# Routing in the merge stage: the router reads the un-normed rows, and its work moves one unit of tiles earlier

## The chip, the cores and the metric

The kernel runs on one core of a Trainium2 chip. The metric is device time in microseconds (us) of one execution; the time before is the median of 3 runs. Engines are named as in the profile: PE is TensorE, DVE VectorE, ACT ScalarE, POOL GpSimd, SP SyncE, which here only issues DMAs.

## The reference

One transformer layer over 1024 prompt rows and 32 sample rows, all float32. Attention and a linear recurrence give two branch outputs o_a and o_b of 512 columns each; they are projected to 1024 columns, gated, and added to x. Then comes a two-level mixture of 32 experts. The part that the change touches is this:

```
proj  = einsum('blnc,ncd->blnd', branches, w_out)
gates = sigmoid(gate_logits)
x  = x + sum(gates * proj, over the 2 branches)
h2 = rmsnorm(x, norm_ffn_g)               # x * rsqrt(mean(x*x) + eps) * g
g_prob = softmax(h2 @ w_rg + b_rg);  g_top, g_idx = top_k(g_prob, 1)
e_logits = h2 @ w_re + b_re;  e_top, e_idx = top_k(e_logits of that group, 2)
e_w = softmax(e_top) * g_top              # weights of the two experts
x  = x + sum over the two experts of e_w * ffn_e(h2)
```

## The kernel before

The program is written out by hand, engine by engine: each engine has its own list in program order, and semaphores (`wait_ge`, `then_inc`) tie them. An instruction that waits holds up all that stands behind it on its engine. The stages follow one another: inputs, mixing, attention, merge, experts.

**The merge** handles 9 tiles of 128 rows. Tile 0 is the tail with the sample rows, tiles 1 to 8 are the prompt. For tile t, PE turns the branch outputs (`turn_o`, L1920), and multiplies them in four units (`project(t, u)`, L1947) of four 512-column matmuls (float32, so each shows as two in the trace). DVE multiplies each unit by its gate (L1720) and adds it to x (L1722); the add of unit 3 raises `x_done`. ACT then sums the squares of x (L1868), DVE scales and adds epsilon (L1744), ACT takes the root (L1870), DVE the reciprocal (L1746) and writes h2 = x * r * g (L1749, `h2_ready`). PE turns h2 (`turn_h2`, L1956), DVE and ACT each copy half of the turned tile from PSUM (L1753, L1874), PE computes 36 logits per row (`router`, L1963), DVE picks the group and the experts (`choose`, L1759 to L1784), PE counts rows per expert before each row (`count`, L1970 to L1980), and DVE turns that into places (`record`, L1791 to L1804). After the last tile `finish_table` (L1810 to L1814) gives the row numbers from which POOL gathers the experts' rows of h2.

**Order on PE** in the loop (L1997): project(t,0), count(t-2), project(t,1), turn_h2(t-1), turn_o(t+1), project(t,2), router(t-1), project(t,3). The router of tile t-1 thus runs inside tile t.

**Order on ACT** (L1893): the squares and root of tile t-1, the sigmoid of the gates of tile t+1 (`sigmoid`, L1863, over 2048 columns), the copy of the turned h2, the copy of the turned branch outputs of tile t+1 (L1858), and `weights(t-1)` (L1879, L1881).

**Gates.** There are two gate buffers. The gates of tile t+1 go into the buffer of tile t-1, so SP loads them (L1628, 1 MB) only after `x_done` of tile t-1, right behind the store of that x (L1637). SP then waits for h2 and stores it (L1641), loads a later x (L1633), in tiles 1 to 3 the weights of an expert (L1644, L1647, 3 MB), and the branch outputs of a later tile (L1621, L1624). After the last projection and the last store of h2 it issues the weights that go into memory the merge used: 2 MB and three times 1 MB.

**The experts** start with gathers by indirect DMA (L2189), issued by POOL once the row numbers stand; PE turns the gathered rows and runs 32 experts.

## Time and profile before

| | us |
|---|---|
| three runs | 1634.65, 1632.19, 1633.59 |
| median | 1633.59 |
| span of the profiled execution | 1634.6 |
| that execution's own time | 1634.65 |
| merge: first turning to row numbers | 1105.5 to 1287.9 |
| PE busy over the whole span | 1502.0 (92%) |

The span starts with the first instruction and ends with the last. Times in the rows are microseconds from its start. In a timeline a bracket at the end of a row tells how long the engine sat idle before it and what released it. The profiled execution is the first of the three runs.

### The profile page before, as it was taken

Reading aid. Unit: us, or ns where it says so; the run is one execution under the profiler, and the core shown is the slowest. Engines: PE = TensorE matmul, PEld = TensorE weight load, DVE = VectorE, ACT = ScalarE, POOL = GpSimd, SP = SyncE. Lnnn points to the kernel's source line nnn. Section 1 sums busy time; section 2 is a strip of 40 time slices with the busy share of each in tenths; the row PEclk is TensorE's granted clock in tenths of the full one; section 3 lists DMA queues with packets and bytes.
Section 4 is the critical chain, followed back from the end, with each engine's and each line's share of the span. In section 5 each row is a group of like instructions: output and inputs, shape, how many; then the busy total and the mean of one; then the engine's idle time right before and its main releaser. Section 6 shows DMA issues by size and latency. Waiting matters only on the chain. (4 is left out here: it accounts for less than half of the span.)

```text
span 1634.6 us, 38777 instructions
## 1 busy us (share of the span) xinstructions
PE 1502.0 (92%) x16352; PEld 1064.2 (65%) x16352; DVE 857.1 (52%) x1874; ACT 446.4 (27%) x882; POOL 102.1 (6%) x102
## 2 busy tenths in 40 slices
PE   6999999969999999999999599988999599999994
PEld 5888888844666666666667466663455477777762
DVE  3555554545566667676776566663777323221211
ACT  2222222223222332333231144433543211111110
POOL 0000000000000000000000000000000122333321
PEclk9999999979999999999999699998999699999998
DMA  9422221544141232212112424436963799999972
GB/s 339 166 91 94 90 90 64 197 139 159 60 128 64 87 94 88 66 62 83 59 47 73 115 61 95 102 77 229 373 231 130 268 313 339 343 346 360 343 244 42
DMA packets 101326, 259.55 MB, mean 159 GB/s; under 512 B 34240, under 2 KB 53328, under 8 KB 91824
## 3 DMA queue, kind: packets, MB, share of 16 engines
q1 hardware_dynamic: 93424, 239.92, 42.8%
q0 software_dynamic: 7744, 17.33, 4.5%
q8 instruction: 124, 2.03, 0.5%
q14 instruction: 34, 0.28, 0.1%
HBM read 205.32 MB, written 60.56 MB: 163 GB/s over the span
## 5 line engine op out<-in xcount | busy, mean ns | idle before, releaser
L540 PEld LDWEIGHTS a_ps<-a_hT,a_wz 128*128 128x128 f32 x1792 | 202.6, 192 | 6.3 <-issue 3.8
L540 PE MATMUL a_ps<-a_hT,a_wz 128*128 128x128 f32 x1792 | 204.1, 275 | 1.8 <-DMA a_wz<-w_z 1.8
L1947 PE MATMUL d_ps<-late,last_down 128*128 128x512 f32 x256 | 115.4, 598 | 1.5 <-DVE last_down L1711 0.8
L2313 DVE TENSOR_SCALAR f_y<-f_down,table 96x512 f32<-96x512 f32 x32 | 23.9, 747 | 123.0 <-PE f_down L2108 70.8
L2115 DVE COPY f_xT<-f_turned 128x384 f32<-128x384 f32 x32 | 17.9, 558 | 123.8 <-PE f_turned L2082 121.2
L1947 PEld LDWEIGHTS d_ps<-late,last_down 128*128 128x128 f32 x256 | 46.7, 190 | 51.5 <-issue 50.2
L1120 PE MATMUL b_ps<-r_wg,r_hT 128*128 128x512 f32 x128 | 66.0, 650 | 12.1 <-POOL b_S L778 10.1
L1472 ACT ACTIVATE late<-c_score,c_top 128x1024 f32<-128x1024 f32 (+8 forms) x72 | 50.7, 704 | 92.8 <-DVE c_top L1421 92.0
L840 DVE TENSOR_TENSOR b_M<-b_ps,r_causal 128x512 f32<-128x512 f32 x72 | 46.4, 686 | 54.8 <-PE b_ps L1181 54.3
L1120 PE MATMUL b_ps<-b_wg,b_hT 128*128 128x512 f32 x128 | 64.2, 624 | 0.9 <-DMA b_hT<-hT_d 0.9
L1120 PE MATMUL b_ps<-b_wg,r_hT 128*128 128x512 f32 x128 | 63.1, 615 | 0.0
L2108 PE MATMUL f_down<-wd,f_midT 128*96 128x512 f32 x136 | 61.3, 593 | 1.8 <-DVE f_midT L2127 1.8
L1271 PE MATMUL b_solve<-b_L,b_U 64*64 64x32 f32 x1408 | 57.1, 222 | 5.7 <-DVE b_L L916 5.4
L1120 PE MATMUL b_ps<-r_wg,b_hT 128*128 128x512 f32 x128 | 62.1, 611 | 0.0
L1271 PEld LDWEIGHTS b_solve<-b_L,b_U 64*64 64x64 f32 x1408 | 51.3, 136 | 13.6 <-DVE b_L L916 6.5
L2320 ACT ACTIVATE f_xT<-f_turned 128x384 f32<-128x384 f32 x32 | 15.7, 492 | 159.7 <-PE f_turned L2082 156.4
L916 DVE TENSOR_TENSOR b_L<-b_solve,r_merge_mask 128x256 f32<-128x256 f32 x44 | 18.7, 424 | 75.3 <-PE b_solve L1255 75.3
L452 ACT ACTIVATE a_z<-a_ps 128x512 f32<-128x512 f32 (+1 forms) x36 | 19.6, 544 | 140.9 <-PE a_ps L540 134.1
L1255 PEld LDWEIGHTS b_solve<-b_T,b_M 64*64 64x64 f32 x1408 | 44.5, 134 | 18.4 <-issue 7.8
L2338 ACT ACTIVATE f_y<-f_down,table 96x512 f32<-96x512 f32 x32 | 21.9, 686 | 126.4 <-PE f_down L2108 73.6
L1519 PE MATMUL c_turned<-c_ident,late 128*128 128x128 f32 (+1 forms) x304 | 49.9, 290 | 6.3 <-ACT late L1472 6.3
L2232 POOL DMA_INDIRECT out<-f_y,rows x32 | 46.3, 1446 | 142.9 <-DVE f_y L2313 139.2
(373 smaller groups left out, 2928.5 us busy)
## 6 DMA issues: line engine op xcount, KB each, us to landing
wgu<-w_gate_up SPq DMA_DIRECT2D x15, 2048.0 KB
late<-w_gate_up SPq DMA_DIRECT2D x9, 2048.0 KB
wd<-w_down SPq DMA_DIRECT2D x17, 1024.0 KB
late<-w_down SPq DMA_DIRECT2D x10, 1024.0 KB
r_hT<-hT_d SPq DMA_DIRECT2D x18, 512.0 KB, 4.0
b_hT<-hT_d SPq DMA_DIRECT2D x18, 512.0 KB, 4.0
gate_d<-b_logits SPq DMA_DIRECT2D x32, 256.0 KB, 2.6
late<-gate_d SPq DMA_DIRECT2D x8, 1024.0 KB, 5.7
```

Of the source, the lines that this page charges most:

```text
L540: mm = pe.matmul(banks[Z_BANKS[n % 2]][:, j * P:(j + 1) * P], wz[:, i, (g + j) * P:(g + j + 1) * P], hT[t % 2][:, i, :], start=(i == 0), s ...
L840: ins = dve.tensor_tensor(m[:, 2 * p + j], banks[(C0, C1)[j]][:].rearrange("p (a b) -> p a b", a=2), spread(causal[:].unsqueeze(1), [P, 2, ...
L1120: mm = pe.matmul(banks[FILLS[q % 2]][:], hT[q % 2][:, k, :], wg[u % 2][:, k, :], start=(k == 0), stop=(k == DC - 1))
L1255: mm = pe.matmul(solve[half, s // 4, s % 4 * Q:s % 4 * Q + Q], m[half, h, 0, half], left, start=True, stop=True)
L1271: mm = pe.matmul(out(1), u[half, s, :], lo[half, s, 0:Q], start=True, stop=True)
L1472: act.activation(probs[b][:, 0:width[s]], score[b][:].rearrange("p a n -> p (a n)")[:, 0:width[s]], ACT.Exp, bias=top[:, b:b + 1], accum_o ...
L1519: mm = pe.transpose(turned[banks_of(p)[n // 4]][0:m, n % 4 * P:(n % 4 + 1) * P], probs[b][:, n * P:n * P + m], ident[:])
L1947: mm = pe.matmul(banks[2 + u][:], oT[t % 2][:, HB * branch(u) + k, :], wo[:, HB * branch(u) + k, half(u)], start=(k == 0), stop=(k == HB - 1))
L2108: mm = pe.matmul(down[h][0:CAP, :], midT[b][:, k, :], wd[wb][:, k, 512 * h:512 * h + 512], start=(k == 0), stop=(k == FB - 1))
L2232: pool.indirect_dma_start(out_rows, bass.IndirectOffsetOnAxis(ap=rows[:, ORDER[e]:ORDER[e] + 1], axis=0), y[e % 2][:], None, bounds_check= ...
L2313: dve.tensor_scalar(y[e % 2][:, 512:], down[1][0:CAP, :], weights[:, ORDER[e]:ORDER[e] + 1], None, ALU.mult).then_inc(s["y_dve"], 1)
L2338: act.activation(y[e % 2][:, 0:512], down[0][0:CAP, :], ACT.Copy, scale=weights[:, ORDER[e]:ORDER[e] + 1]).then_inc(s["y_act"], 1)
```

## The change

The router no longer reads h2. In `merge`, at its start, DVE multiplies the router's weights by the norm's gain g (one instruction over 288 columns; g comes as columns, by one more small DMA). PE turns x itself (`turn_x`, L1973 of the new file) as soon as `x_done` is raised; the row's factor r is applied to the logits when DVE adds the bias (L1766). h2 is still computed, for the experts, in `norm` (L1754), but nothing on PE waits for it. `mean_square` is split from `norm`, so that `record(t-2)` runs between the two.

The weights of the two experts are computed with Exp alone: with d = e_top[1] - e_top[0], the first is 1 / ((1 + exp d) * sum) and the second that times exp d. Before, Sigmoid was used. A one-element Exp stands first in `weights`.

The orders are rewritten. On PE the turning of x(t-1) comes behind project(t,0), the router of t-1 behind project(t,1), and the count of t-1 at the end of tile t. For the last tile, turning goes to the PSUM banks 0 and 1, and the count of tile 7 stands in the middle of project(8,3).

PE in the middle of the merge, one tile of the loop, before (names: `late` and `last_down` hold the output weights and the turned branch outputs, `seventh` x or h2, `unit` the identity):

```order
L1947 MATMUL d_ps<-late,last_down 128x512 x8
L1970 MATMUL d_ps<-d_both,m_before 128x32
L1971 MATMUL d_ps<-d_both,d_ones 128x32
L1980 MATMUL d_ps<-d_told,d_at_place 96x64 x2
L1947 MATMUL d_ps<-late,last_down 128x512 x4
L1956 MATMUL d_ps<-unit,seventh 128x128 x8
L1920 MATMUL d_ps<-unit,late 128x128 x8
L1947 MATMUL d_ps<-late,last_down 128x512 x4
L1963 MATMUL d_ps<-m_wr,d_h2T 64x36 x16
```

The same engine and place after the change:

```order
L1961 MATMUL d_ps<-late,last_down 128x512 x4
L1973 MATMUL d_ps<-unit,seventh 128x128 x8
L1961 MATMUL d_ps<-late,last_down 128x512 x4
L1980 MATMUL d_ps<-m_wr,d_xT 64x36 x16
L1932 MATMUL d_ps<-unit,late 128x128 x8
L1961 MATMUL d_ps<-late,last_down 128x512 x8
L1988 MATMUL d_ps<-d_both,m_before 128x32
L1989 MATMUL d_ps<-d_both,d_ones 128x32
L1998 MATMUL d_ps<-d_told,d_at_place 96x64 x2
```

The same instructions are there. Turning has moved ahead of project(t,1); between turning and the router there stands project(t,1), where turn_o(t+1) and project(t,2) stood before.

ACT in one tile of the loop, before (L1870 is the root, L1863 the sigmoid of the gates, L1874 the copy of the turned tile):

```order
L1870 ACTIVATE d_ms<-d_ms 128x1
L1863 ACT_TABLE_LOAD
L1863 ACTIVATE late<-late 128x2048
L1874 ACTIVATE d_h2T<-d_ps 128x512
L1858 ACTIVATE last_down<-d_ps 128x512
L1879 ACTIVATE d_small<-d_small 128x2
L1881 ACT_TABLE_LOAD
L1881 ACTIVATE d_gexp,d_small<-d_lg,d_small 128x4
L1866 ACT_TABLE_LOAD
L1866 ACTIVATE d_root_ready<-d_ones 128x1
```

And after:

```order
L1880 ACTIVATE d_ms<-d_ms 128x1
L1873 ACT_TABLE_LOAD
L1873 ACTIVATE late<-late 128x2048
L1885 ACTIVATE d_xT<-d_ps 128x512
L1868 ACTIVATE last_down<-d_ps 128x512
L1889 ACT_TABLE_LOAD
L1889 ACTIVATE d_exp_ready<-d_ones 128x1
L1891 ACTIVATE d_gexp,d_small<-d_lg,d_small 128x4
L1893 ACTIVATE d_small<-d_small 128x1
L1876 ACT_TABLE_LOAD
L1876 ACTIVATE d_root_ready<-d_ones 128x1
```

The copy of the turned tile keeps its place behind the sigmoid; the table load for Exp now stands before any wait of `weights`.

PE at the end of the merge, after the change, from project(8,3):

```order
L1961 MATMUL d_ps<-late,last_down 128x512 x6
L1988 MATMUL d_ps<-d_both,m_before 128x32
L1989 MATMUL d_ps<-d_both,d_ones 128x32
L1998 MATMUL d_ps<-d_told,d_at_place 96x64 x2
L1961 MATMUL d_ps<-late,last_down 128x512 x2
L1973 MATMUL d_ps<-unit,seventh 128x128 x8
L1980 MATMUL d_ps<-m_wr,d_xT 64x36 x16
```

Before, the count of tile 7 stood behind all of project(8,3). The core of the diff:

```diff
@@ SP
             def load_x(t):
                 after(sp, x_stored[t % 3], 16 * (t // 3))
                 after(sp, h2_ready, t - 2)
+                after(sp, xT_done, t - 2)
@@ DVE
-            def norm(n):
+            def mean_square(n):
                 col = ms[:, n:n + 1]
                 dve.wait_ge(x_sq, n + 1)
                 dve.tensor_scalar(col, col, 1.0 / D, EPS, ALU.mult, ALU.add).then_inc(ms_ready, 1)
+
+            def norm(n):
+                col = ms[:, n:n + 1]
                 dve.wait_ge(rms_root, n + 1)
                 step(dve.reciprocal(col, col))
                 after(dve, h2_stored[n % 2], 16 * (n // 2))
-                after(dve, h2T_done, n - 1)
...
-                dve.tensor_tensor(lg[:], banks[6][:, 0:RT], br[:], ALU.add).then_inc(lg_copied, 1)
+                after(dve, g_sum, n)
+                dve.scalar_tensor_tensor(lg[:], turned_into(n)[0][:, 0:RT], ms[:, n:n + 1], br[:], ALU.mult, ALU.add).then_inc(lg_copied, 1)
...
             mix_tail()
+            step(dve.tensor_tensor(wr[:], wr[:], spread(g_cols[:].unsqueeze(2), [P, DC, RT]), ALU.mult))
             copy_oT(1)
...
             for t in range(2, NT):
                 step.lap()
+                mean_square(t - 1)
+                record(t - 2)
                 norm(t - 1)
-                if t == 2:
-                    record(0)
                 unit(t, 0)
-                if t > 2:
-                    record(t - 2)
+                copy_xT(t - 1)
                 unit(t, 1)
-                copy_h2T(t - 1)
                 if t + 1 < NT:
                     copy_oT(t + 1)
+                choose(t - 1)
                 unit(t, 2)
-                choose(t - 1)
+                if t == NT - 1:
+                    record(t - 1)
                 unit(t, 3)
+            mean_square(NT - 1)
+            copy_xT(NT - 1)
             norm(NT - 1)
-            record(NT - 2)
-            copy_h2T(NT - 1)
             choose(NT - 1)
             record(NT - 1)
@@ ACT, weights(n)
-                act.wait_ge(d_ready, n + 1)
-                act.activation(sm[:, 6:8], sm[:, 4:6], ACT.Sigmoid).then_inc(d_sig, 1)
+                act.activation(exp_ready[:], ones[:, 0:1], ACT.Exp)
                 act.wait_ge(neg_top, n + 1)
                 act.activation(gexp[:], lg[:, 0:NG], ACT.Exp, bias=sm[:, 0:1], accum_out=sm[:, 1:2]).then_inc(g_sum, 1)
+                act.wait_ge(d_ready, n + 1)
+                act.activation(sm[:, 6:7], sm[:, 5:6], ACT.Exp).then_inc(d_exp, 1)
@@ PE
-            def turn_h2(n):
-                pe.wait_ge(h2_ready, n + 1)
-                after(pe, counted, n)
-                after(pe, lg_copied, n)
+            def turn_x(n):
+                pe.wait_ge(x_done, n + 1)
+                if n < NT - 1:
+                    after(pe, counted, n)
+                    after(pe, lg_copied, n)
+                else:
+                    pe.wait_ge(oT_copied, 2 * NT)
...
             project(1, 1)
+            turn_x(0)
             project(1, 2)
-            turn_h2(0)
+            router(0)
             project(1, 3)
-            router(0)
```

## Rows read from the trace of the kernel before

**Rows 1.** The page: the chain that ended last, by line

```profile
PE f_down L2108 7%; PE d_ps L1947 6%; PE f_gated L2097 6%; PE f_upped L2097 5%; PE f_turned L2082 2%; PE d_ps L1956 1%; PE d_ps L1963 1%; PE d_ps L1920 0%; PE d_ps L1928 0%; DMA xg<-h_d,rows 0%; PE d_ps L1980 0%; DMA late<-oa_d 0%; DVE seventh L1749 0%; ACT L1866 0%
```

**Rows 2.** The chain in order of time, one tile: start us, us, what

```profile
1217.42 3.49 PE d_ps L1947 x8
1220.91 0.78 issue
1221.69 1.06 PE d_ps L1956 x8
1222.76 0.87 PE d_ps L1920 x8
1223.63 3.44 PE d_ps L1947 x8
1227.06 1.06 PE d_ps L1963 x32
1228.12 7.06 PE d_ps L1947 x16
...
1235.92 3.49 PE d_ps L1947 x8
```

**Rows 3.** DVE's timeline: start us, us, line, operation, [idle before]

```profile
1159.26 0.69 DVE L1722 TENSOR_TENSOR seventh<-seventh,d_mixed 128x512 f32<-128x512 f32 x1
...
1214.13 0.69 DVE L1722 TENSOR_TENSOR seventh<-seventh,d_mixed 128x512 f32<-128x512 f32 x1
...
1250.99 0.69 DVE L1722 TENSOR_TENSOR seventh<-seventh,d_mixed 128x512 f32<-128x512 f32 x1
...
1268.47 0.69 DVE L1722 TENSOR_TENSOR seventh<-seventh,d_mixed 128x512 f32<-128x512 f32 x1
```

**Rows 4.** ACT's timeline

```profile
1151.29 1.91 ACT L1863 ACTIVATE late<-late 128x2048 f32<-128x2048 f32 x1 [4.58 <-DMA late<-gate_d]
...
1220.92 1.92 ACT L1863 ACTIVATE late<-late 128x2048 f32<-128x2048 f32 x1 [1.91 <-DMA late<-gate_d]
1222.79 0.60 ACT L1874 ACTIVATE d_h2T<-d_ps 128x512 f32<-128x512 f32 x1
...
1270.48 1.04 ACT L1868 ACTIVATE d_junk<-seventh 128x1024 f32<-128x1024 f32 x1
```

**Rows 5.** SP's timeline: DMA issues

```profile
1273.95 0.43 SPq L1644 DMA_DIRECT2D late<-w_gate_up  x1
```

**Rows 6.** Issue to landing, gates issued at 1125.01, then at 1215.24

```profile
late<-gate_d SPq DMA_DIRECT2D x1, 1024.0 KB, 5.4
...
late<-gate_d SPq DMA_DIRECT2D x1, 1024.0 KB, 5.7
```

**Rows 7.** The chain in order of time, end of the merge

```profile
1272.27 1.30 DVE seventh L1749
...
1274.44 1.95 PE d_ps L1956 x8
...
1277.23 1.95 PE d_ps L1963 x32
...
1279.20 0.21 DVE d_lg L1759
...
1282.71 0.64 PE d_ps L1970 x2
...
1284.51 0.20 DVE d_pos L1795
...
1287.72 0.19 DVE rows L1814
...
1288.90 4.34 DMA xg<-h_d,rows
```

**Rows 8.** Stretches: us, busy by engine, PEclk (granted clock), DMA share, GB/s

```profile
1268.00:1269.20 1.20, 0.90 (x8) 0.76 (x8) 1.13 (x2) 1.17 (x4) 1.20 (x2) 1.00 0.00 0
1280.00:1288.00 8.00, 2.63 (x12) 2.29 (x12) 4.96 (x28) 1.88 (x4) 0.00 (x0) 0.50 0.99 421
```

More of the change, by code:

```diff
@@ L1562, in merge @@
         wo, begun = keep["wo"], keep["begun"]
-        wr, br, ident, before, g_ffn, count_up, real, token, places, nobody, fold = (begun[n] for n in "wr br ident before g_ffn count_up real token places nobody fold".split())
+        wr, br, ident, before, g_ffn, count_up, real, token, places, nobody, fold, g_cols = (begun[n] for n in "wr br ident before g_ffn count_up real token places nobody fold g_cols".split())
         ones = sb("ones", [P, P])
@@ L1747, in norm, with copy_xT @@
                 after(dve, h2_stored[n % 2], 16 * (n // 2))
-                after(dve, h2T_done, n - 1)
                 dve.scalar_tensor_tensor(h2[n % 2][:], x[n % 3][:], col, g_ffn[:], ALU.mult, ALU.mult).then_inc(h2_ready, 1)
-            def copy_h2T(n):
-                dve.wait_ge(h2T_done, n + 1)
-                dve.tensor_copy(h2T[:, 4:, :], banks[7][:].rearrange("p (a b) -> p a b", b=P)).then_inc(h2T_copied, 1)
+            def copy_xT(n):
+                dve.wait_ge(xT_done, n + 1)
+                after(dve, lg_done, n)
+                dve.tensor_copy(xT[:, 4:, :], turned_into(n)[1][:].rearrange("p (a b) -> p a b", b=P)).then_inc(xT_copied, 1)
             def choose(n):
@@ L1790, in record @@
                 dve.wait_ge(g_sum, n + 1)
-                step(dve.reciprocal(sm[:, 3:4], sm[:, 1:2]))
-                dve.wait_ge(d_sig, n + 1)
-                dve.tensor_scalar(rec[:, 2 * NE + 4:], sm[:, 6:8], sm[:, 3:4], None, ALU.mult)
+                dve.wait_ge(d_exp, n + 1)
+                step(dve.scalar_tensor_tensor(sm[:, 3:4], sm[:, 6:7], 1.0, sm[:, 1:2], ALU.add, ALU.mult))
+                step(dve.reciprocal(rec[:, 2 * NE + 4:2 * NE + 5], sm[:, 3:4]))
+                dve.tensor_tensor(rec[:, 2 * NE + 5:], rec[:, 2 * NE + 4:2 * NE + 5], sm[:, 6:7], ALU.mult)
                 dve.wait_ge(count_done, n + 1)
@@ L1824, in _ @@
             unit(1, 1)
+            mean_square(0)
             norm(0)
             copy_oT(2)
+            copy_xT(0)
             unit(1, 2)
-            copy_h2T(0)
             unit(1, 3)
@@ L1870, in norm, with copy_xT @@
                 act.activation(ms[:, n:n + 1], ms[:, n:n + 1], ACT.Sqrt).then_inc(rms_root, 1)
[L1872 to L1874 removed]
+            def copy_xT(n):
+                act.wait_ge(xT_done, n + 1)
+                after(act, lg_done, n)
+                act.activation(xT[:, 0:4, :], turned_into(n)[0][:].rearrange("p (a b) -> p a b", b=P), ACT.Copy).then_inc(xT_copied, 1)
             def weights(n):
                 sm = small[n % 2]
[L1878 to L1879 removed]
+                act.activation(exp_ready[:], ones[:, 0:1], ACT.Exp)
                 act.wait_ge(neg_top, n + 1)
                 act.activation(gexp[:], lg[:, 0:NG], ACT.Exp, bias=sm[:, 0:1], accum_out=sm[:, 1:2]).then_inc(g_sum, 1)
+                act.wait_ge(d_ready, n + 1)
+                act.activation(sm[:, 6:7], sm[:, 5:6], ACT.Exp).then_inc(d_exp, 1)
             sigmoid(0)
@@ L1936, in fold_tail, with project @@
                 mm.then_inc(fold_done, 1)
-            def project(t, u):
+            def project(t, u, between=None):
                 pe.wait_ge(oT_copied, 2 * (t + 1))
@@ L1946, in project @@
                 for k in range(HB):
+                    if k == HB // 2 and between is not None:
+                        between()
                     mm = pe.matmul(banks[2 + u][:], oT[t % 2][:, HB * branch(u) + k, :], wo[:, HB * branch(u) + k, half(u)],
@@ L1968, in count @@
                 pe.wait_ge(both_ready, n + 1)
-                pe.wait_ge(h2T_copied, 2 * (n + 1))
+                pe.wait_ge(xT_copied, 2 * (n + 1))
+                after(pe, counted, n)
                 pe.matmul(banks[7][:, 0:NE], before[:], both[:], start=True, stop=True)
@@ L1992, in _ @@
             project(1, 1)
+            turn_x(0)
             project(1, 2)
-            turn_h2(0)
+            router(0)
             project(1, 3)
-            router(0)
             for t in range(2, NT):
-                project(t, 0)
-                count(t - 2)
+                if t == 2:
+                    project(t, 0, lambda: count(0))
+                else:
+                    project(t, 0)
+                turn_x(t - 1)
                 project(t, 1)
-                turn_h2(t - 1)
+                router(t - 1)
                 if t + 1 < NT:
@@ L2004, in _ @@
                 project(t, 2)
-                router(t - 1)
-                project(t, 3)
-            count(NT - 2)
-            turn_h2(NT - 1)
+                if t == NT - 1:
+                    project(t, 3, lambda: count(NT - 2))
+                else:
+                    project(t, 3)
+                    count(t - 1)
+            turn_x(NT - 1)
             router(NT - 1)
```

35 lines of the change are left out of this document (17 added, 18 removed).

## The prediction

> **What bounds the kernel now.** I read the page's chain first [rows 1]: it is nearly all PE, in the experts (L2082, L2097, L2108) and in the merge (L1947 and the turning and routing lines). The change touches only the merge and the start of the experts, so I read the chain there in order of time [rows 2]. One tile lasts from 1217.42 to 1235.92, 18.50 us. Of that 0.78 is a hole ahead of the turning (L1956); the rest, 17.72, is PE at work: four units of about 3.5, turning 1.06, turning o 0.87, routing 1.06, and by difference 0.74 for the count. DVE's adds of unit 3 end (start plus 0.69) at 1159.95 for tile 2 and 1251.68 for tile 7 [rows 3], so five tiles took 91.73, or 18.35 each. The reader should see that PE is 96% full there: all that a better order can win in a tile of the loop is about 0.65 us.
>
> Next come the engines that PE waits for. On ACT the sigmoid of the next tile's gates starts at 1220.92 and was released by the DMA of the gates; the copy of the turned tile follows it at 1222.79 and ends at 1223.39 [rows 4]. Routing started only at 1227.06 [rows 2]: 3.6 us of slack.
>
> Last, the end of the merge [rows 3, 7]: x of tile 8 is complete at 1269.16, the row numbers stand at 1287.91. These 18.75 us are a chain without overlap: squares on ACT from 1270.48 [rows 4], h2, turning 1.95, copy, routing 1.95, choose, count, record. PE's granted clock is 1.00 before and 0.50 in this stretch, the lower level of 1.2 GHz [rows 8], which is why turning takes 1.95 and not 1.06.
>
> **The loop.** PE's instructions per tile stay the same, 17.72 us. What goes is the hole: turning needs `x_done` and the count's release instead of h2. With t0 the moment of `x_done` (PE's last unit ends 1.45 before it, for two DVE instructions of 0.7), PE does the count 0.74 and project(t,0) 3.53, and wants to turn at t0+2.8. DVE's release (`counted`) comes after squares 1.25, mean 0.2 and the first half of record, about 1.1: t0+2.6. No hole there, or a very small one.
>
> Then comes project(t,1), 3.49, and PE wants to route at t0+7.4. The turned tile must have been copied by both engines. DVE gets there after record 2.1, norm 1.5, one unit 1.45 and the copy 0.7, at about t0+7.1. ACT does not. Its copy still stands behind the sigmoid, and the sigmoid behind the gates, whose load cannot be issued before t0, since their buffer is that of tile t-1. From `x_done` at 1214.82 the sigmoid started 6.10 later [rows 3, 4], the load having taken 5.7 from issue [rows 6]. After the change h2 is stored later, so the gates have the queue to themselves as at 1125.01, where the load took 5.4: 5.80. Then sigmoid 1.87, copy 0.60 and a signal 0.05: routing starts at t0+8.3. The slack of 3.6 is used up because turn_o and project(t,2), 4.3 together, no longer stand in front of routing; PE waits about 0.95.
>
> So the tile becomes a ring through the DMA: 8.32, routing 1.06, turn_o 0.87, two units 3.44 and 3.53, and 1.45 to the next `x_done`: 18.67, against 18.35. Five tiles (3 to 7) cost 5 x 0.32 = 1.6 us instead of winning 3. The bounds of the landing are the two rows, 5.4 and 5.7: ring 18.67 to 18.97, or 1.6 to 3.1 in all; below, I allow 0.2 less landing for a queue quieter still, 0.6. I take 1.6.
>
> **The first tiles.** The gates of tile 3 landed so that the sigmoid ran at 1151.29 [rows 4]; their load stood behind 3 MB of expert weights, which are issued after h2 of tile 0, a step that is not moved. So this time stays. The copy ends at 1153.8, where routing began before too. But then turn_o and project(2,2) had been done, now they come after it. `x_done` of tile 2 is 1153.80+1.06+0.87+3.44+3.53+1.45 = 1164.15 instead of 1159.95: +4.2. The longer wait for choose(0) ahead of the count inside project(2,0), about 3.6, lies in the shadow of these gates. Bounds: +2.7 if the queue is emptied earlier by 1.5, +5.7 if later.
>
> **The last tile of the loop** has no gates to load: 17.6 us from `x_done` to `x_done`, now with the count of tile 7 inside, against 17.5 (1251.68 to 1269.16). Together `x_done` of tile 8 comes 4.2+1.6+0.1 = 5.9 later.
>
> **The end.** From `x_done` of tile 8: squares 1.25, mean 0.2, root 0.25, ACT's copy 0.6, routing 1.06 end at 3.4; DVE meanwhile copies 0.7, takes the reciprocal 0.2 and writes h2 1.3 [rows 7], free at 3.6. Choose takes what it took from 1279.20 to 1282.71, 3.5; the count until 1284.51, 1.8; the rest until 1287.91, 3.4. Sum 12.3 against 18.75: 6.45 won. It is what stood in series before: turning, one of its copies and h2, the Exp with its table load ahead of the squares (ACT began them at 1270.48, 1.3 after x was there), and turning and routing at the lower clock. PE now rests about 1.5 us before turning, so I take 1.06 for each. If the clock falls all the same, 0.9 comes back on the routing; if it stays at 1.00 through the count as well, 1.3 more is won.
>
> **The start.** One DVE multiply over 288 columns stands ahead of the copy of turned branch outputs; scaled from 0.69 for 512 columns it takes 0.4, of which some lies in a short wait. I take 0.2, bounds 0 and 0.4. The constant's DMA lies under attention, at nothing; if that cover were missing it would be one small load before the merge.
>
> **The gather.** The weights into freed memory, 5 MB, are issued once h2 of tile 8 is stored. Before, that was 1273.95 [rows 5], and at 421 GB/s and a DMA share of 0.99 [rows 8] they were through as the gather began at 1288.90, which landed 4.34 later [rows 7]. Now the store comes 3.6 after `x_done` instead of 4.4, and the row numbers 12.3 after it instead of 18.75. The gather begins 5 to 6 us before the weights are through. Lower bound nothing; upper bound: it waits for them all, landing at 18.9+3.2 = 22.1 after `x_done` instead of 17.6, +4.5. I take 2.0, nearer the lower end, for the gather is small (96 rows) and on another queue.
>
> The Trainium skill, "DMA: Bandwidth & Descriptors", section "Queues, rings and completion order", says that each DMA engine goes round among its queues, one packet at a time. By that rule the gather shares instead of waiting, which favours the lower half of my bounds; no row here shows a gather's landing beside a full weight queue.
>
> **Sum.** Start +0.2, tiles +5.9, end -6.45, gather +2.0: +1.65. The profiled execution took 1634.65, 1.06 above the median of the three, so the sum is 1636.3 on its scale and 1635.2 on the median's. The experts behind carry it one for one: their weight loads are released by their own steps.
>
> Another page bears on the end. Rows show the table loads as 1.28 each, with the next instruction right behind. The Trainium skill, "ScalarE: Activation LUTs", section "What ACT_TABLE_LOAD costs", gives 2.66 for every switch, a drain of 1.38 included. By it, taking a load out of the end would win 1.38 more, 1633.8 in all. The rows disagree and decide.
>
> **Rivals.** First, faster: the gates do not hold PE. It would need the copy ready at t0+7.4, a landing 0.95 shorter than the 5.4 seen; then five waits go, -4.8, and the median is 1630.4, or 1628.4 with a free gather. For it: 1.5 MB are moved, and the queue is quieter; against it: even the undisturbed load took 5.4. Second, slower: the gather waits for the weights to the end, +2.5 on my term, 1637.7. For it: the share of 0.99 over the whole stretch; it decides as soon as more than 4.3 us of weights stand before the gather. Third, slower: the gates of tile 4 or 5 queue behind the 3 MB of weights that are now issued later, after the later h2. Those weights need about 12 us from some 5 after `x_done`, and the next `x_done` comes at 18.7, so about 1.5 us are to spare; if that is gone one or two tiles lose 1 to 3 us, 1638.0. Fourth, the change does not do what it says: `counted` comes late and turning is not earlier. It has a margin of 0.2 only, but a delay below 0.95 vanishes in the wait for the gates, so this gives the forecast's time.
>
> **How the numbers follow.** Forecast 0.52 (the fourth rival is in it), first rival 0.18, second 0.16, third 0.14. A measurement of this kernel tells about 0.2%, 3.3 us, from no change: 1630.3 to 1636.9. The forecast's own range is 1632 to 1638; I count 0.42 of it as same, 0.08 as slower, 0.02 as faster. The first rival gives faster 0.14 and same 0.04; the second slower 0.12, same 0.04; the third slower 0.10, same 0.04. Rounded: faster 0.17, same 0.53, slower 0.30. The range of 1629.5 to 1639.5 takes in the upper half of the first rival and nearly all of the others.
>
> **What would show it.** In the trace after: L1980 (routing) on PE has a wait of about 1 us in tiles 3 to 7 that ends with ACT's copy L1885, itself right behind the sigmoid L1873 released by the DMA of gates; no hole before L1973; the adds of unit 3 lie 18.7 apart; routing of tile 1 starts near 1153.8; from the last such add to the row numbers 12.3 us; the first gather lands more than 5 us after its start. I am wrong if routing starts right behind project(t,1), or if the end saves less than 5 us.

## The result and the profile after

The changed kernel takes 1642.42 us, median of 6 runs (1638.67 to 1647.53); the kernel before, run beside it, 1633.74 (1628.85 to 1634.88). The ratio is 1.0063, with a 95% interval of 1.0048 to 1.0078: slower by 8.7 us by the medians and by 10 by the ratio, where no measurable change was forecast. It lies above the range of 1629.5 to 1639.5. The profiled execution took 1642.85, its span is 1641.0.

All stretches below are counted from the start of `project(1, 0)`, the first full unit of the merge (1117.76 before, 1113.32 after). Of the change only the multiply lies ahead of it: it runs 0.45 us (1112.09), and PE's wait there is 0.99 instead of 0.78. Otherwise this start varies between single executions: in the profiles of all kernels here it lies between 1112.7 and 1117.8. So absolute times of two profiles can't be compared. From there to the end the profiles show 516.84 us before and 527.68 after, 10.8 more; the two spans differ by only 6.4, since the part ahead happened to be 4.4 shorter in the second.

The page of the profile, the chain by line, answers to [rows 1]. New in it, against the kernel before, are the DMA of the gates and ACT's copy:

```profile
PE f_down L2131 7%; PE f_gated L2120 6%; PE f_upped L2120 5%; PE d_ps L1961 5%; DMA late<-gate_d 2%; PE f_turned L2105 2%; PE d_ps L1980 1%; PE d_ps L1932 0%; DMA xg<-h_d,rows 0%; PE d_ps L1940 0%; DVE d_mixed L1723 0%; DVE seventh L1725 0%; ACT d_xT L1885 0%; DMA late<-oa_d 0%
```

The chain in order of time (start us, us, what) over one tile, the answer to [rows 2]. L1725 is the last add of a unit (`x_done`), L1640 and `late<-gate_d` the store of x and the load of the gates, L1885 ACT's copy, L1980 routing, L1932 `turn_o`:

```profile
1201.04 0.70 DVE seventh L1725
...
1201.76 0.34 SPq L1640
...
1202.14 5.63 DMA late<-gate_d
...
1207.91 1.71 issue
1209.61 0.59 ACT d_xT L1885
...
1210.25 1.13 PE d_ps L1980 x32
1211.38 1.02 PE d_ps L1932 x8
1212.40 6.88 PE d_ps L1961 x16
...
1219.38 0.70 DVE d_mixed L1723
...
1220.10 0.70 DVE seventh L1725
```

This is the ring that the prediction describes, from one `x_done` to the next through the gates' DMA: 19.06 us, where [rows 2] have 18.50 with PE at work. (The 1.71 of "issue" is the sigmoid, which runs from 1207.80.) DVE's timeline, the last add of tiles 2, 3, 7 and 8, answers to [rows 3]:

```profile
1161.48 0.69 DVE L1725 TENSOR_TENSOR seventh<-seventh,d_mixed 128x512 f32<-128x512 f32 x1
...
1182.18 0.69 DVE L1725 TENSOR_TENSOR m_x<-m_x,d_mixed 128x512 f32<-128x512 f32 x1
...
1258.29 0.69 DVE L1725 TENSOR_TENSOR seventh<-seventh,d_mixed 128x512 f32<-128x512 f32 x1
...
1275.72 0.69 DVE L1725 TENSOR_TENSOR seventh<-seventh,d_mixed 128x512 f32<-128x512 f32 x1
```

Tile 3 took 20.70, the four behind it 19.03 each, (1258.29 - 1182.18) / 4. PE's timeline with its waits (start us, us, line, [idle before <- releaser]) shows what happened up to tile 3:

```profile
1130.10 1.15 PE L1980 MATMUL d_ps<-m_wr,d_xT 128*64 128x36 f32 x32 [1.81 <-ACT d_xT L1885]
...
1141.93 0.63 PE L1988 MATMUL d_ps<-d_both,m_before 128*128 128x32 f32 x2 [3.70 <-DVE d_both L1791]
...
1142.80 3.76 PE L1961 MATMUL d_ps<-late,last_down 128*128 128x512 f32 x4
1146.36 1.92 PE L1973 MATMUL d_ps<-unit,seventh 128*128 128x128 f32 x8
...
1151.63 1.13 PE L1980 MATMUL d_ps<-m_wr,d_xT 128*64 128x36 f32 x32
...
1170.64 1.13 PE L1980 MATMUL d_ps<-m_wr,d_xT 128*64 128x36 f32 x32 [1.46 <-ACT d_xT L1885]
1171.70 1.70 PE L1932 MATMUL d_ps<-unit,late 128*128 128x128 f32 x8
```

PE waited 1.81 ahead of routing(0) and 3.70 inside `project(2, 0)` for choose(0). Four matmuls behind the second wait took 3.76, half a unit, which at full speed is 1.8; turning took 1.92 instead of 1.04. The same behind the wait of 1.46: `turn_o` 1.70 instead of 1.09. The windows (us, busy by engine, granted clock, DMA share, GB/s) show what changed there:

```profile
1130.00:1134.00 4.00, 3.90 (x36) 2.28 (x37) 0.00 (x0) 1.53 (x3) 0.00 (x0) 0.63 1.03 392
...
1140.00:1148.00 8.00, 6.07 (x16) 3.90 (x17) 5.87 (x26) 5.86 (x8) 0.00 (x0) 0.58 0.59 233
...
1172.00:1174.00 2.00, 2.00 (x9) 1.53 (x8) 0.50 (x1) 0.56 (x1) 0.00 (x0) 0.51 0.96 356
...
1180.00:1268.00 88.00, 82.10 (x423) 44.31 (x422) 60.72 (x196) 39.77 (x62) 0.00 (x0) 1.00 0.50 179
```

The granted clock fell from 1.00 (2.4 GHz) to 0.50 (1.2 GHz) for a few us behind these three rests, and not behind the four of 1.3 to 1.6 that came later. The kernel before rests 1.85 us at 1145.8 and keeps 1.00 behind it, so the length of a rest alone does not decide it. Last, the end of the merge in the chain, the answer to [rows 7]:

```profile
1277.93 0.59 ACT d_xT L1885
1278.57 1.95 PE d_ps L1980 x32
1280.55 0.27 DVE d_lg L1766
...
1284.11 0.64 PE d_ps L1988 x2
...
1285.91 0.20 DVE d_pos L1803
...
1289.13 0.19 DVE rows L1822
...
1290.31 7.69 DMA xg<-h_d,rows
```

and SP's timeline there, the answer to [rows 5]:

```profile
1279.83 0.32 SPq L1644 DMA_DIRECT2D h_d<-seventh  x1
1280.19 0.43 SPq L1647 DMA_DIRECT2D late<-w_gate_up  x1
```

Row numbers stand 12.9 us after the last `x_done` (18.75 before). But the late weights (5 MB) are issued 10.1 us before the gather instead of 15.0, and the gather takes 7.69 instead of 4.34. The windows show what runs beside it, at its start and its end:

```profile
1290.00:1292.00 2.00, 0.00 (x0) 0.00 (x0) 0.00 (x0) 0.00 (x0) 1.39 (x2) 0.50 1.01 426
...
1296.00:1298.00 2.00, 0.00 (x0) 0.00 (x0) 0.00 (x0) 0.00 (x0) 0.00 (x0) 0.50 0.79 189
```

By an estimate the weights, if nothing else ran, would be through some 4 us after the gather's start (5.77 MB with h2's store, at 421 GB/s [rows 8] 13.7 us from the issue at 1279.83, and some 0.7 until the first bytes in the trace of the DMA engines: 1294.2). Counted by queue in steps of 0.5 us, the gather's first bytes move 4.0 to 4.5 us after its start, against 1.5 to 2.0 in the kernel before; the weights' last ones move 5.0 to 5.5 after it.

The account over the stretches, in us against before:

| stretch | forecast | measured |
|---|---|---|
| multiply, ahead of `project(1, 0)` | +0.2 | +0.2 |
| start of `project(1, 0)` to `x_done` of tile 2 | +4.2 | +6.7 |
| tiles 3 to 7 | +1.6 | +5.1 |
| tile 8 | +0.1 | -0.05 |
| `x_done` of tile 8 to row numbers | -6.45 | -5.8 |
| gather, to the experts' first turning | +2.0 | +3.4 |
| experts | 0 | +1.6 |
| sum | +1.65 | +11.0 |

### The profile page after: what moved, and what is told of

Same layout as the page of the kernel before. It is cut to its first block and busy times, and to the rows that moved or that the text cites. A ratio compares the mean times of both kernels' runs of the same rounds, so it can differ in the third digit from the quotient of the medians.

```text
span 1641.0 us, 38805 instructions
## 1 busy us (share of the span) xinstructions
PE 1503.4 (92%) x16352; PEld 1067.1 (65%) x16352; DVE 857.9 (52%) x1884; ACT 445.1 (27%) x889; POOL 102.0 (6%) x102
## 5 line engine op out<-in xcount | busy, mean ns | idle before, releaser
L1961 PE MATMUL d_ps<-late,last_down 128*128 128x512 f32 x256 | 119.6, 615 | 1.7 <-DVE last_down L1714 1.0
L1120 PE MATMUL b_ps<-r_wg,r_hT 128*128 128x512 f32 x128 | 64.8, 640 | 12.1 <-POOL b_S L778 10.3
```

Source lines behind the costliest of these rows:

```text
L1120: mm = pe.matmul(banks[FILLS[q % 2]][:], hT[q % 2][:, k, :], wg[u % 2][:, k, :], start=(k == 0), stop=(k == DC - 1))
L1961: mm = pe.matmul(banks[2 + u][:], oT[t % 2][:, HB * branch(u) + k, :], wo[:, HB * branch(u) + k, half(u)], start=(k == 0), stop=(k == HB - 1))
```

## The experiments

Theory: two things were mis-sized, the ring through the gates and rests of PE that cost more than their own length because the clock falls behind them; and the gather is slow because weights run beside it. Rival for the first: the loads queue behind each other on SP, so their order decides. Every kernel below is the changed one with the edit shown, but for one.

**Copy ahead of the sigmoid.** In ACT's loop:

```diff
-                if t + 1 < NT:
-                    sigmoid(t + 1)
                 copy_xT(t - 1)
                 if t + 1 < NT:
+                    sigmoid(t + 1)
                     copy_oT(t + 1)
```

> The changed kernel with one edit: in the merge's loop ACT copies the turned x(t-1) ahead of the sigmoid of the gates of tile t+1 instead of behind it. Ring theory (PE's wait before routing ends with ACT's copy, which stands behind the DMA of the gates and the sigmoid): the waits of 1.3 to 1.6 us before L1980 in tiles 3 to 7 (7.4 us in all) go, the five tiles take about 88.7 us instead of 96.8, and the kernel 7 to 9 us less than the changed one. Rival (DVE, with record, norm and its own copy, is what routing waits for): the waits stay within 0.3 us of what they are. Second rival (what was lost is PE's clock, not the wait): the tiles of 19.1 us stay.

Measured: 1630.68 us, ratio 0.9979 (0.9962 to 0.9997) to before, 11.7 us less than the changed kernel by the medians, where 7 to 9 were expected (by the ratios 3.4 below before, and 8 to 13 above for the changed one). In PE's timeline of this kernel routing has no wait, and `turn_o` behind it runs at full speed:

```profile
1202.20 1.13 PE L1979 MATMUL d_ps<-m_wr,d_xT 128*64 128x36 f32 x32
1203.26 1.09 PE L1931 MATMUL d_ps<-unit,late 128*128 128x128 f32 x8
```

The tiles take 17.48 each, less than before the change (18.35). The ring is shown: it stood in the order of two instructions on ACT. The waits of 1.81 and 3.71 in tiles 1 and 2 stayed, and with them 5.1 of the 6.7 us lost there. The other 1.6 is not the edit's: behind the same wait of 1.81 the clock stayed at 1.00 in this execution. Row numbers stand 5.9 us earlier than before the change, but the gather takes 9.06, and the experts' first turning comes only 1.2 us earlier.

**Routing behind the third unit.** `router(t - 1)` on PE moves from behind `project(t, 1)` to behind `project(t, 2)`, and `choose(t - 1)` on DVE to behind `unit(t, 2)`, for all but the last tile of the loop.

> The changed kernel with the router of tile t-1 put back behind turn_o(t+1) and project(t,2) in tiles 2 to 7 (and choose behind unit 2 on DVE), all else as changed. Ring theory: routing has 4.3 us more slack than it needs, no wait for the copy, five tiles about 88.7 us, and in tile 2, too, routing no longer holds up project(2,2); 7 to 9 us less than the changed kernel. Rival (earlier turning itself, or choose on DVE, costs the time): no gain, or a new hole before x_done.

Measured: 1635.56, ratio 1.0018 (1.0001 to 1.0036); a tile takes 18.16, five 90.8 where 88.7 were expected. ACT's copy now has the slack of one unit, as in the kernel before. PE waits 0.37 per tile for choose instead. The first stretch kept its whole loss (49.01), against the expectation. Row numbers stand where they stood before (169.9 after the start, 170.1 before), and the gather of 9.16 is what is left of the loss.

**Gates ahead of the store of x** on SP, `load_logits(t + 2)` and `store_x(t)` exchanged.

> The changed kernel with SP's two DMAs behind x_done exchanged: the gates of tile t+1 (1 MB) are issued ahead of the store of x (0.5 MB). Ring theory: the gates land about 0.4 (one issue) plus 1.3 (0.5 MB at 0.37 MB per us) earlier after x_done, the sigmoid and with it the copy too, and the waits before routing of 1.3 to 1.6 us nearly vanish: five tiles about 89 to 90 us, 6 to 8 us less in all. Rival (DVE's copy or the clock): no change in the waits, whatever the gates do.

Measured: 1641.12, ratio 1.0045 (1.0028 to 1.0062). My expectation failed. The issues of this kernel (KB each, median us from issue to landing), 1195 to 1212:

```profile
late<-gate_d SPq DMA_DIRECT2D x1, 1024.0 KB, 6.0
out<-seventh SPq DMA_DIRECT2D x1, 512.0 KB, 6.9
```

In the changed kernel, with the store issued first, the same view has the gates at 5.6 and the store at 2.9. First in the queue does not mean alone: the 0.4 us won at issue is lost in landing, and the waits of 1.2 to 1.5 stay. What costs the gates time is that 512 KB more are moved within the same microseconds; the next kernel shows it. The Trainium skill, "DMA: Bandwidth & Descriptors", section "Queues, rings and completion order", says that completion is not first in, first out per issuing engine. These rows do not test it: in both kernels the two transfers landed in the order in which they were issued.

**Gates alone.** The store of x moves behind the store of h2:

```diff
-                store_x(t)
                 if t + 2 < NT:
                     load_logits(t + 2)
                 store_h2(t)
+                store_x(t)
```

> The changed kernel, with one edit: in each tile SP issues the store of x behind the gates and behind the store of h2, so nothing else is on the way when the gates of the tile after next are loaded. Exchanging the two alone had moved nothing: the gates landed 5.8 us after issue either way, and the store took the rest. Theory of the ring (five tiles of 19.36 us each are a chain of x_done, load of the gates, sigmoid, ACT's copy, routing): the load alone takes 4.0 to 4.5 us instead of 5.6, the waits of 1.3 to 1.6 us before routing in tiles 3 to 7 go, the clock doesn't fall there, a tile takes 17.5 to 17.8, and x_done of tile 8 comes 7 to 9 us earlier: 1633 to 1636 us. Rival, the load takes its 5.6 us whatever is beside it (its 1 MB packets and its own completion set it): waits and times as in the changed kernel, 1641 to 1643. A second rival, the later store of x holds up the load of x (three buffers): a new wait of DVE on x in some tiles.

Measured: 1636.01, ratio 1.0017 (1.0002 to 1.0032), just at the upper end of what was expected. The gates land faster; one row of the issues, 1198 to 1215, and PE's routing behind them:

```profile
late<-gate_d SPq DMA_DIRECT2D x1, 1024.0 KB, 4.7
```

```profile
1193.39 1.13 PE L1980 MATMUL d_ps<-m_wr,d_xT 128*64 128x36 f32 x32 [2.36 <-ACT d_xT L1885]
...
1211.13 1.13 PE L1980 MATMUL d_ps<-m_wr,d_xT 128*64 128x36 f32 x32 [0.19 <-ACT d_xT L1885]
```

Tiles take 17.7 to 18.0, but one had a wait of 2.36 and took 19.9; its gates landed after 6.9. So the wait follows the landing: what the landing exceeds about 4.5 PE waits, in all five tiles of this kernel (landings 4.7 to 6.9, waits 0.19 to 2.36). The rest of 2.36 cost its own length and no more: the granted clock was 1.00 in 1193 to 1203.

**Count moved.** In tile 2 `count(0)` stands behind `project(2, 1)`, ahead of `turn_x(1)`, and `router(1)` behind `project(2, 2)`; DVE's `unit(2, 2)` ahead of `choose(1)`.

> The changed kernel with tile 2 alone reordered: project(2,0), project(2,1), then count(0), turn_x(1), turn_o(3), project(2,2), router(1), so that PE does not wait 3.7 us for choose(0) in the middle of project(2,0). Clock theory (x_done of tile 2 came 2.5 us later than I forecast because PE rested 3.7 us and its granted clock was 0.50 for the next 6 us): clock 1.00 there, x_done of tile 2 comes 5 to 7 us earlier relative to the start of the merge, which includes routing moved off the wait for the gates; the time falls by 4 to 7 us. Rival (the gates of tile 3 set that point, as I forecast): x_done of tile 2 moves by less than 2.5 us.

Measured: 1641.19, ratio 1.0047 (1.0026 to 1.0068). `x_done` of tile 2 came 6.5 us earlier (42.31 instead of 48.85 after the start), which is the loss of the first stretch. Some 1.7 of these 6.5 came ahead of the edit, since here, too, the clock stayed at 1.00 behind the wait of 1.81. In the profile 2.6 us were left at `x_done` of tile 8 (160.54 instead of 163.09), and the time can't be told from that of the changed kernel, where 4 to 7 us less were expected. ACT's sigmoid of tile 4 and PE's routing in this kernel:

```profile
1163.39 1.91 ACT L1876 ACTIVATE late<-late 128x2048 f32<-128x2048 f32 x1 [5.41 <-DMA late<-gate_d]
```

```profile
1165.84 1.25 PE L1983 MATMUL d_ps<-m_wr,d_xT 128*64 128x36 f32 x32 [3.24 <-ACT d_xT L1888]
1167.02 1.97 PE L1935 MATMUL d_ps<-unit,late 128*128 128x128 f32 x8
```

An earlier `x_done` only meets the 3 MB of expert weights that are still in the queue, the gates land late, PE waits 3.24 and the clock falls behind it: that tile took 22.93. Another, with a wait of 1.61, took 20.85, again with a fall. The prediction's third rival (gates queued behind late weights) is met, but once tile 2 is early, not where it is late.

**PE kept busy.** Products that nobody reads: two matmuls of 512 columns ahead of `router(0)`, four inside `project(2, 0)` ahead of `count(0)`. All waits and all real work stay; one wait, for the bank that the four write, is new.

> The changed kernel, with one addition: where PE rests in the first tiles it multiplies something that nobody reads, two matmuls of 512 columns (0.87 each) ahead of routing(0), where it waited 1.81 us, and four inside project(2,0) ahead of count(0), where it waited 3.70. They write banks that the next real product starts anew. The work and all waits stay otherwise. Theory of the clock: the 6.7 us lost up to x_done of tile 2 came with a granted clock of 0.50 after these two waits, not from the waits; kept busy, PE stays at 1.00 in 1132 to 1150 and x_done of tile 2 comes 2.5 to 4 us earlier (4.2 later than before instead of 6.7, as the sum in the prediction had it), the rest as in the changed kernel: 1638 to 1640 us. Rival, the waits themselves and the gates set it: no difference, 1641 to 1643, or slower where the additions run past the waits.

Measured: 1640.17, ratio 1.0038 (1.0017 to 1.0060), just beyond the 1638 to 1640 expected. `x_done` of tile 2 stands at 46.68 instead of 48.85, 4.5 later than before where the prediction had 4.2. And now the wait that the prediction had seen there appears in PE's timeline:

```profile
1149.75 1.13 PE L1980 MATMUL d_ps<-m_wr,d_xT 128*64 128x36 f32 x32 [1.99 <-ACT d_xT L1885]
```

In the changed kernel PE had been too slow to meet it (1151.63 has no wait). Behind it the clock stays at 1.00. But two later tiles of this run took 20.8 instead of 19, with the granted clock at 0.65 in 1190 to 1194.

**PE kept busy in each tile.** The same, and one such matmul ahead of each routing of the loop.

> The changed kernel with products that nobody reads in the places where PE rests: two ahead of routing(0), four inside project(2,0), and one (0.87 us) ahead of each routing of the loop, where PE waited 1.3 to 1.6. In the kernel with those of the first two places alone x_done of tile 2 came 2.2 us earlier, as the theory of the clock had it, but two later tiles took 20.8 instead of 19. Theory: these two, and the tile of 20.7 in the changed kernel, are falls of the clock to 0.50 after the short waits; with PE kept busy all tiles of the loop take 18.8 to 19.1, the clock stays at 1.00 from 1132 to 1274, and the kernel takes 1637 to 1638.5. Rival: the falls have another cause (the load behind a long tile, chance): tiles of 20.7 stay, 1640 to 1642.

Measured: 1638.49, ratio 1.0044 (1.0027 to 1.0061). The window of its loop, from tile 2 on:

```profile
1152.00:1268.00 116.00, 112.90 (x542) 59.72 (x541) 81.15 (x276) 53.70 (x88) 0.00 (x0) 1.00 0.61 224
```

The clock stays at 1.00, in 1116 to 1152 too, and tiles 3 to 7 take 18.80 to 19.32, none over 20; tile 8, whose routing had no wait to fill, takes 18.30, 0.9 more. The two kernels with additions show the clock's share: 2.2 us in tiles 1 and 2, and 1.7 to 1.9 in each tile in which it falls. With more work on PE the row numbers come earlier in the profile, at 172.28 instead of 175.99. In the time this is not shown: the interval overlaps with that of the changed kernel.

**Late weights behind the gather.** SP waits for the first gather before it issues the last 5 MB (the expectation says 4):

```diff
             sp.wait_ge(proj_done, units_before(NT))
+            sp.wait_ge(keep["gathered"]["x_in0"], 16)
             load_up(LATE[0])
```

> The changed kernel, with one edit: the weights of the two late experts (all of them but one load, 4 MB) are issued only once the first gather has landed. Theory: the gather's 7.69 us (4.34 before) were the weights that ran beside it, so it lands in 4.2 to 4.6 again, 3.1 to 3.5 us earlier. The weights start some 16 us later than now; if the experts behind have that to spare the kernel takes 1638.5 to 1639.5 us. Rival A: the gather is slow because the stores of h2 and x or PE's state stand beside it, and stays at 7 to 8: no change or slower. Rival B: the experts' weight loads are one queue without slack, and the later start comes back at the last experts (waits on up weights): the gather is short, the stretch from the first turning of the experts to the end is 4 us or more longer than 343, and nothing is won, 1642 to 1646.

Measured: 1651.75, ratio 1.0124 (1.0093 to 1.0155). The gather is short, as the theory has it, and the experts pay for it. The chain's row, and two of PE's waits over the experts:

```profile
1287.65 4.45 DMA xg<-h_d,rows
```

```profile
PE f_upped L2121 <- issue: 4.5, 3, 2.1
PE f_gated L2121 <- DMA wgu<-w_gate_up: 3.8, 3, 1.4
```

From the first turning to the end it takes 353.96 instead of 342.95. Between 1300 and 1540 the DMA share is 0.97 to 1.02 in every window of 40 us of this kernel, and 0.88 to 1.02 in the changed one: the experts' weights are one stream with hardly a gap, and what is issued 12 us late comes back as waits from 1470 on: between 1460 and 1540 PE is idle for 8.1 us, in the changed kernel for none. One such window of the changed kernel:

```profile
1380.00:1420.00 40.00, 40.00 (x612) 30.00 (x610) 11.16 (x39) 5.57 (x12) 10.63 (x10) 1.00 1.02 345
```

PE and the DMA engines are both full there. Rival B was right, with 11 us instead of my "4 or more", and the time lies above its 1642 to 1646. The rests that the profile calls "issue", 4.5 us, have no releaser there; what they are stays open.

**The kernel before, late weights held.** `sp.wait_ge(lg_done, NT)` ahead of the same loads in the kernel before.

> The kernel before, with one edit: the same late weights wait until the last tile has been routed, 5.3 us later than now and so as close ahead of the gather (some 9 us) as in the changed kernel. Theory of contention: the gather of the kernel before takes 7 to 8 us instead of 4.34, with nothing of the change in it, and the kernel takes 3 us longer: 1636 to 1637.5. Rival, the changed routing itself makes the gather slow: it stays at 4.3 to 4.6 and the time at 1633 to 1634.

Measured: 1635.62, ratio 1.0021 (1.0005 to 1.0038): 3.4 us more, a little below the 1636 to 1637.5 expected.

```profile
1285.32 7.91 DMA xg<-h_d,rows
```

The gather takes 7.91 instead of 4.34 [rows 7] with nothing of the change in the kernel: the weights beside it are the cause, and the new routing has a part in it only by its timing.

**Late weights earlier.** The last tile's h2 and x are stored from ACT's queue, so SP does not wait for h2.

> The changed kernel, with one edit: the last tile's h2 and x are stored by ACT's queue, so SP no longer waits for h2 and issues the 4 MB of late weights as soon as the last projection is through, some 5 us earlier, without delaying them as the kernel did that held them behind the gather. Theory of contention: some 5 us more of the weights are through when the gather starts, and it takes 4.3 to 5.5 instead of 7.7, 2.5 to 3.3 us won, with the experts' stretch at 341 to 343: 1638 to 1639.5. Rival: the stores of h2 and x now share with the weights and land later, and the gather waits for the stores as long as it gains: 1641 to 1643.

Measured: 1639.59, ratio 1.0036 (1.0020 to 1.0052). From its chain:

```profile
1281.84 12.11 DMA out<-seventh
...
1295.18 4.46 DMA xg<-h_d,rows
```

The gather is clean at 4.46, but it starts 5.1 us after the row numbers: GpSimd waits for the store of x, which now takes 12.11 beside the weights (2.9 for such a store inside the loop). The contention was moved to another transfer: from the last `x_done` to the experts' first turning it takes 21.66, in the changed kernel 21.64. The rival's mechanism was right, though the time is below its 1641 to 1643. What this kernel is faster in the profile, 4.9 us from the start of `project(1, 0)`, lies in the loop and the experts: 1.5 up to `x_done` of tile 8, since none of its tiles had a fall of the clock, and 3.3 in the experts (339.6). By the intervals the two times can't be told apart.

**Copy and count together.** The first edit, also for tile 0, with the fourth.

> Two edits of the changed kernel together: ACT copies the turned tile ahead of the sigmoid of the tile after next, also for tile 0 (so routing never waits for gates), and in tile 2 the count of tile 0 stands behind project(2,1) instead of inside project(2,0) (so PE doesn't rest 3.7 us there). If the two losses are independent, x_done of tile 2 comes 42.3 us after the start of the first full unit (42.2 before, 48.9 in the changed kernel), the six tiles behind take 17.5 each, x_done of tile 8 147.3 (151.4 before, 163.1 changed), the row numbers 159.4; the gather starts some 4 us closer to the weights than before and takes 9, the experts turn at 169.5 to 170 instead of 175.5: 1627 to 1629 us. Rival: the gates of tile 4 stand behind 3 MB of expert weights, as they did when the count alone was moved (a tile of 22.9 us there), and one tile loses 2 to 5 us: 1630 to 1633. Second rival: the experts' stretch is bound by its weights, which are not issued as much earlier, and it takes 3 us more than its 341.

Measured: 1623.01, ratio 0.9947 (0.9931 to 0.9964): 9.9 us faster than the kernel before by the medians, 8.7 by the ratio, and the lowest of all. `x_done` of tile 2 at 40.95 (42.19 before), tile 3 at 18.00, the four behind it 17.48 each. From DVE's timeline, tiles 4 and 7:

```profile
1188.67 0.69 DVE L1725 TENSOR_TENSOR seventh<-seventh,d_mixed 128x512 f32<-128x512 f32 x1
...
1241.11 0.69 DVE L1725 TENSOR_TENSOR seventh<-seventh,d_mixed 128x512 f32<-128x512 f32 x1
```

The gates of tile 4 still queue behind 3 MB of weights, which cost 4 us when the count alone was moved; with the copy ahead only the sigmoid is late, and tile 3 loses 0.5. The gather starts 9.3 us after the late weights' issue and takes

```profile
1272.32 9.62 DMA xg<-h_d,rows
```

so of the 11.8 us by which the row numbers are earlier (158.39 against 170.14) 6.5 reach the experts. My forecast was 4 to 6 us too high: tile 2 came 1.4 earlier than I had it, and the experts took 338.8, not 341; the rest is not accounted for.

**All three edits.**

> Copy ahead of the sigmoid, count of tile 0 moved, and the late weights issued earlier with the last stores on ACT's queue: all three edits. From the parts: row numbers at 159.4 after the start of the first full unit (170.1 before), gather 4.5 to 6, experts' first turning at 165 to 166.5 (175.5 before, 184.7 changed): 9 to 10.5 us before the kernel before if its experts take their 341 us, 1622 to 1625. If the experts' weights are the bound, less: 1625 to 1628.

Measured: 1626.23, ratio 0.9960 (0.9944 to 0.9975), above the two alone but within overlapping intervals, though in its profile the experts' first turning comes at 166.87 after the start instead of 169.05. In the profiles the part ahead of the merge differs by 2.6 us against it (1115.55 and 1112.93); neither a loss nor a gain by the third edit is shown. The store of x took 11.45, and the gather behind it 4.14.

## Why the prediction was wrong

Most mechanisms were the right ones: turning has no hole, the ring through the gates sets the tile, routing waits for ACT's copy, the end is shorter by about what was worked out, and the gather meets the weights. What was missing is what a rest can do to PE's clock. Of the sizes, all but that of tile 8 were wrong in the same direction. With every term at the upper bound that the prediction gives it (start 0.4, tile 2 5.7, five tiles 3.1, last tile 0.1, end -5.55 with the slow routing, gather 4.5) the sum is +8.25 and the time 1641.8, near the measured one; the range ended at 1639.5, since the upper bounds were never put together. But that agreement is luck: term by term the table has +11.0, with tiles 1 to 7 and the experts beyond their bounds and the end and the gather within theirs, and a part ahead of the merge that happened to be shorter makes up for it.

- **Tiles 1 and 2**, +6.7 against +4.2. The step that failed is "The longer wait for choose(0) ... lies in the shadow of these gates". It did in the sense of waiting; but PE came out of it at 0.50 of its clock, ran half a unit and the turning 2.8 us slower, on top of some 1.7 lost by the clock behind the wait of 1.81, and reached routing(1) 2.7 after the gates' tile was copied (1148.91). With PE kept busy the sum of the prediction comes out (+4.5, with the gates' wait of 1.99 visible). A rest was priced at its length, and the half speed behind it was left out: that term was put at nothing without a reason. It is no fixed price: the clock fell behind the wait of 3.7 in all seven kernels that have it, behind the 1.81 in six of eight.
- **Tiles 3 to 7**, +5.1 against +1.6: the largest miss. The ring was right, its terms short by 0.39 per tile (19.06 - 18.67), 1.9 in five: 0.23 of each is the gates' landing, 5.63 instead of 5.4, since the store of x goes with them. The step was that "the gates have the queue to themselves", which held for h2 and not for x. The other 0.16 is spread over PE's and DVE's pieces. One tile cost 1.6 more by the clock's fall behind its wait of 1.46, which the prediction had at 0.95 and priced at that. This 1.6 is partly the single execution's: the loops of the kernels with the late weights behind the gather and with the late weights earlier are the changed kernel's, and none of their tiles had a fall (`x_done` of tile 8 at 161.5 instead of 163.1).
- **The first rival** (gates do not hold PE) was named at 0.18 and would need a landing 0.95 shorter. The kernel with the gates alone shows it nearly reached at 4.7.
- **The end**, -5.8 against -6.45. Routing ran at the lower clock, 1.95, though the prediction took 1.06 for "PE now rests about 1.5 us before turning". It had named the 0.9 as the cost if the clock falls; that branch came true here. In seven of the other kernels with the same end (1.58 and 1.0 of rest) the clock was not down at routing, which took 1.13, and the end took 12.1, against 12.3 in the prediction.
- **The gather**, +3.4 against +2.0. That the weights are the cause is shown from both sides (4.45 without them, 7.91 with them in the kernel before). The size that failed is the choice of the lower end, "for the gather is small (96 rows) and on another queue". The delay over 4.34 is about as long as weights are left at the gather's start, each worked out as above: changed kernel 3.9 left, 3.35 late; kernel before with late weights 3.5 left (5.24 MB, 12.4 us and 0.7 from 1275.66, to 1288.8), 3.57 late; copy and count 4.7 left (13.7 and 0.7 from h2's store at 1262.65), 5.28 late. That comes close to the second rival, with less before it than its 5 to 6 us, but it is not its mechanism: in every kernel here with weights beside the gather its first bytes move 4.0 to 4.5 us after its start, whether 3.5 or 4.7 us of weights are left, and 1.5 to 2.0 where none are; from then on both queues move bytes, for 1 to 3.5 us. So the gather loses some 2.5 us before its first byte, and the rest while both queues move. The Trainium skill, "DMA: Bandwidth & Descriptors", section "Queues, rings and completion order", has each engine go round among its queues by packets, and I leaned on it. By an equal share the gather's 0.39 MB (96 rows of 4 KB) would, as an estimate, cost about 1 us more at 421 GB/s; the runs show 3.35 to 5.28. The measurement decides; why the first bytes come so late was not tested.
- **The experts**, +1.6 against 0. "The experts behind carry it one for one" holds within 1 to 3 us only: this stretch took 338.8 to 343.0 in all kernels but the one that issues late, 354. Its weights are the second bound of the kernel, which the chain, full of PE, did not show; the windows' DMA share does. The 1.6 here are about what PE waits longer for gate weights in the last experts, 5.3 us in four waits from 1571 on against 3.6 in three before.

The chances were off too: slower had 0.30, by the second and third rivals. The third did not occur in the changed kernel and the second only in part; the clock behind the rests ahead of `x_done` of tile 8 was in no rival.

## What to carry to other kernels

When a step is moved up on one engine, follow each of its inputs through the in-order queue of the other: here a copy of 0.6 us stood behind a sigmoid that waits for a DMA, and exchanging the two turned some 10 us lost into 3 won, and with the count's move into 9 won. Give a rest of the tensor engine two prices, its length and its length with a few us of half speed behind it (here 1.6 to 2.8 us more): the one of 3.7 us always cost the second, those of 1.2 to 2.4 sometimes. Place steps so that rests are filled or vanish. Where a stage ends with a small transfer on the critical path and a large prefetch is due at the same time, winning time ahead of it brings the two together: count what is left of the prefetch, and whether the stage behind can spare it, before booking the gain.

## What the runs showed of the hardware that I had not expected

- The order of two transfers on one queue made little difference to the one that mattered: gates first 6.0 us, gates second 5.6 (and issued 0.4 later); with nothing beside them 4.7. The 512 KB store went from 2.9 to 6.9.
- Beside 5 MB of weights on their way a store of 512 KB on ACT's queue took 11.45 to 12.11 instead of 2.9, and the gather of 96 rows 7.69 to 9.62 instead of 4.1 to 4.5. In the gather's case the first bytes moved 4.0 to 4.5 us after its start instead of 1.5 to 2.0.
- Behind 29 rests of 1.2 to 1.9 us ahead of routing in tiles 3 to 7, in six kernels, the granted clock fell five times: once each in the changed kernel, with the gates first and with the count moved, twice with PE kept busy in the first tiles, and never with the late weights behind the gather or earlier. Rests of 1.85 (kernel before), 1.99 and 2.36 were followed by 1.00, those of 3.24 and 3.7 by 0.50. What tells the short ones apart was not found.
